# One third of a conditioning matrix in two halves, and another third moved to the end of the layer before

## The chip, the cores and the metric

The kernel runs on one core of a Trainium2 chip. The metric is the device time of one execution in microseconds (us); the median of three runs of the kernel before is 1125.9 us (1125.2 to 1128.83).

## The reference: what is computed

Two layers over 640 tokens (512 latent, 128 context) of width 1024. Cut to what matters here:

```python
mod = silu(c) @ w_ada[l] + b_ada[l]          # one row for latent, one for context: 6*1024 columns
shift1, scale1, gate1, shift2, scale2, gate2 = split(mod, 6)
h = rms_norm(x, norm1) * (1 + scale1) + shift1
proj = h @ w_in                              # 1024 -> 2048, then attention, gating MLP, convolution
x = x + gate1 * (merged @ w_out)
h2 = rms_norm(x, norm2) * (1 + scale2) + shift2
x = x + gate2 * hierarchical_moe(h2, ...)    # two experts of sixteen for each token
```

The weight `w_ada[l]` is 1024 x 6144 floats, 25 MB a layer. Its columns are used in three thirds: the first is shift1 and scale1 (wanted before the layer's first matmul), the second gate1 and shift2, the third scale2 and gate2 (wanted after the attention).

## The kernel before

All work is written out by hand, one instruction stream for each engine, ordered by semaphores; there is no planner. Tokens are five tiles of 128 (four latent, one context). Float32 products are made of three passes (`three`, L1421 to L1423): weights and activations are split into a high and a low part (ScalarE makes `wH`, `actH`; VectorE `wL`, `actL`).

**The weight stream.** `STREAM` lists the 1 MB units of w_ada ("ada"), w_in and w_out ("w") in the order in which SP loads them. They share four buffers (`raw`, RAWS = 4), so unit i+4 is issued only when unit i has been read (`unit_used`). SP is one queue in program order; parameter loads, convolution shifts and expert loads stand in the same queue.

**A modulation unit** (`ada_mm`, L1439) is four matmuls of a 128 x 32 slice of silu(c) with 512 columns each, into four groups of 32 rows of one PSUM bank. Eight units make a third. VectorE adds the bias (`piece_add`, or `half_add` after each four units), GpSimd loads the biases (`bias_in`, four DMAs) and writes finished thirds to memory (`piece_out`, L495). For the first third TensorE transposes the sums to columns (`modc_cols`, L1447) and VectorE makes shift and scale columns `modc` of it (`modc_out`, L1002 and L1007).

**Start of layer 0.** SP loads four units, then an x tile with each further unit, all eight units ahead of w_in. ScalarE squares the five x tiles (L639), scales them (L645), then splits the first w_in unit (L659). TensorE transposes x (`h_chunk`, L1463); ScalarE applies the columns (L676, L678, L681) and VectorE makes the low part (L1035) for each of eight k-tiles; then the projection runs k-tile by k-tile, 15 matmuls each for the first 512 columns.

**Attention** goes over 40 heads (`u`, five tiles of eight; the context tile comes first as tile 0 with only 128 keys). `ADA_AT` puts the second and last third of the layer's modulation, 16 units, among the heads: four in each of the tiles 0 to 3, at heads 2 to 5. `HALF_AT` puts VectorE's bias additions (L993, L996) at the last head of each of these tiles.

**End of layer 0.** After the experts GpSimd gathers two rows for each token (`y1`, `y2`, ten indirect DMAs of 512 KB, L619). ScalarE scales the first (L946); VectorE combines and adds to x, tile by tile (L1403 to L1405); ScalarE squares and scales x for the next layer. SP's first four loads of layer 1 (w_in units) wait for the fourth tile's gathers (`y_in3`). The first third of layer 1's modulation has been computed earlier, in front of and among the routing of layer 0.

Of the kernel before, what the change touches and what calls it, by code (L numbers as in the profile page):

```python
# [16 lines left out]
P = 128  # L17
D = 1024
# [66 lines left out]
def build(nc, I, O):  # L85
    with ExitStack() as ctx:
# [112 lines left out]

        rt = pool[:, 11264:13312]  # L200
# [41 lines left out]
        ADA_AT = (0, 0, 1, 1, 1, 1, 0, 0) * NLT + (0,) * NH  # L242
        HALF_AT = {8 * t + 7: t for t in range(NLT)}
# [3 lines left out]
        def ada_bank(l, q):  # L247

            return 7 if q else 6 if l else 5
# [22 lines left out]
        def unit_loaded(eng, kind, l, n):  # L272
            i = POS[kind, l, n]
            eng.wait_ge(s_raw[i % RAWS], 16 * (i // RAWS + 1))
# [12 lines left out]
        def _(sp):  # L287
# [30 lines left out]
            def load_taps(l):  # L318

                sp.wait_ge(sem("modc_psum"), at("modc_psum", l, 1))  # L320
# [4 lines left out]
            for l in range(DEPTH):  # L325
                for i in range(START[l], START[l + 1]):
                    kind, ll, n = STREAM[i]
                    if i == START[l] + (20 if l == 0 else 12):
# [31 lines left out]
                    k0, n0 = (n % 2) * 4, (n // 2) * N  # L360
                    if kind == "ada":
# [92 lines left out]
        def _(pl):  # L454
# [24 lines left out]

            def bias_in(l, q):  # L480

                if q == 1:
# [3 lines left out]
                for j in range(4):  # L486
                    c = q * U + j * N
                    pl.dma_start(bpiece[q][32 * j:32 * j + 32, :], I["b_ada"][l, c:c + N].partition_broadcast(32)).then_inc(sem("bias_in"), 16)

            def piece_out(l, q):  # L490

                pl.wait_ge(sem("piece_done"), at("piece_done", l, q + 1))
                for j in range(4):
                    c = q * U + j * N
                    pl.dma_start(modrow[l][:, c:c + N], piece[q][32 * j:32 * j + 2, :]).then_inc(sem("piece_out"), 16)  # L495
# [5 lines left out]
            bias_in(0, 0)  # L501
            rstd1(0)
            first = pairs = 0
            for l in range(DEPTH):
# [10 lines left out]
                bias_in(l, 1)  # L515
# [26 lines left out]
                piece_out(l, 1)  # L542
# [74 lines left out]
                for t in range(NT):  # L617
                    for c, y in enumerate((y1[t], y2[t])):
                        pl.indirect_dma_start(y, None, ys, bass.IndirectOffsetOnAxis(slot[:, c * NT + t:c * NT + t + 1], 0)  # L619
                                              ).then_inc(sem(f"y_in{t}"), 16)  # L620
                rstd1(l + 1)


        @block.scalar
        def _(act):
# [21 lines left out]
            for t in range(NT):  # L647
                act.wait_ge(sem(f"x_loaded{t}"), 16)
                norm1_square(0, t)
            for t in range(NT):  # L650
                norm1_scale(0, t)
            first = pairs = 0
            for l in range(DEPTH):
# [13 lines left out]

                split_hi(0)

                for k in range(KD):  # L670
                    act.wait_ge(sem("hT_psum"), at("hT_psum", l, k + 1))
                    if k == 0:
                        act.wait_ge(sem("a1_ready"), at("a1_ready", l, 1))
                    if k >= 2:
                        act.wait_ge(sem("h_lo"), at("h_lo", l, k - 1))
                    act.activation(hf[:, k % 2, 0:512], ps[:, 5 + 2 * (k % 2), :], ACT.Identity,  # L676
# [24 lines left out]
                for gi in range(4 * NT):  # L701
# [27 lines left out]
                    elif nb == 1:  # L729
                        j = t if t < CTX else CTXK  # L730
                        act.wait_ge(sem("ssqk"), at("ssqk", l, t + 1))
# [224 lines left out]
        def _(dve):  # L956
# [22 lines left out]
            def piece_add(l, q):  # L979

                dve.wait_ge(sem("ada_read"), at("ada_read", l, KD * (q + 1)))
                dve.wait_ge(sem("bias_in"), at("bias_in", l, 64 * (q + 1)))
# [4 lines left out]
            def half_add(l, i):  # L987

                q, half = 1 + i // 2, i % 2
                dve.wait_ge(sem("ada_read"), at("ada_read", l, KD * q + 4 * half + 4))  # L990
                if half == 0:
                    dve.wait_ge(sem("bias_in"), at("bias_in", l, 64 * (q + 1)))
                    dve.tensor_tensor(piece[q], ps[:, ada_bank(l, q), :], bpiece[q], ALU.add).then_inc(sem("piece_half"), 1)  # L993
                else:
                    dve.wait_ge(sem("piece_half"), at("piece_half", l, q))
                    dve.tensor_tensor(piece[q], ps[:, ada_bank(l, q), :], piece[q], ALU.add).then_inc(sem("piece_done"), 1)  # L996

            def modc_out(l):

                dve.wait_ge(sem("modc_psum"), at("modc_psum", l, 1))  # L1000
# [3 lines left out]
                dve.wait_ge(sem("modc_in"), 4 * (l + 1))  # L1004
                if l == 0:
                    dve.wait_ge(sem("norm1_loaded"), 16 * DEPTH)
# [10 lines left out]
            piece_add(0, 0)  # L1017
            modc_out(0)
            first = pairs = 0
            for l in range(DEPTH):  # L1020
# [12 lines left out]
                for k in range(KD):  # L1033
# [3 lines left out]
                    if k == 2:  # L1037
                        split_lo(1)
                split_lo(2)
# [757 lines left out]
```

## Time and profile before

| | us |
|---|---|
| median of three runs | 1125.9 |
| the profiled execution | 1123.17 |
| its span, first to last instruction | 1121.3 |
| TensorE busy | 937.7 (84%) |
| VectorE busy | 674.9 (60%) |
| ScalarE busy | 591.5 (53%) |
| GpSimd busy | 260.7 (23%) |

The page divides the span into 40 slices; in them the DMA engines carry over 400 GB/s while experts are loaded, and 10 to 250 in most others. TensorE is idle or nearly so in three places: the first 44 us, the stretch from 544 to 581 (end of layer 0) and the last 43 us. A stall of an engine off the chain of waits costs nothing by itself.

### The profile page before, as it was taken

To read this page: it belongs to the slowest core of one execution; us is meant where nothing else is said; L and a number is where in the kernel's file an instruction comes from. 1 tells how busy PE (TensorE), PEld (TensorE's weight loads), DVE (VectorE), ACT (ScalarE), POOL (GpSimd) and SP (SyncE) were. 2 spreads that over 40 slices of the span, in tenths; PEclk is the share of its full clock that TensorE was granted. 3 is DMA by queue.
4 is the path that set the end of the run, shared out by engine and by line. 5 is a ranking of instruction groups with operands and counts; after the bars stand their busy time and mean duration, and the time that the engine had idled before them with its cause. 6 is when DMAs were issued, how large, how long until landed. Compare 5 with 4: busy or idle time off the path is not lost.

```text
span 1121.3 us, 15024 instructions
## 1 busy us (share of the span) xinstructions
PE 937.7 (84%) x5232; PEld 733.4 (65%) x5232; DVE 674.9 (60%) x945; ACT 591.5 (53%) x913; POOL 260.7 (23%) x306
## 2 busy tenths in 40 slices
PE   3799998996999599999329999899789939999920
PEld 0488874765778278888218888467668838888710
DVE  0249315565264699999273941455725669998936
ACT  1662225565232288888275322556623418888732
POOL 3015006212041122220240410620203212222143
PEclk9999998999997699999759999999989959999975
DMA  9956216643153999999771240566313449999853
GB/s 318 285 184 245 75 59 222 242 152 115 56 216 113 381 332 406 418 413 369 185 283 43 77 149 10 202 236 226 113 58 132 158 155 347 400 421 405 342 196 122
DMA packets 85951, 248.36 MB, mean 221 GB/s; under 512 B 25644, under 2 KB 30252, under 8 KB 75656
## 3 DMA queue, kind: packets, MB, share of 16 engines
q1 hardware_dynamic: 72760, 209.54, 50.2%
q0 software_dynamic: 11696, 32.86, 8.5%
q10 hardware_dynamic: 1440, 5.24, 1.2%
q8 instruction: 33, 0.54, 0.2%
q14 instruction: 22, 0.18, 0.0%
HBM read 221.07 MB, written 30.21 MB: 224 GB/s over the span
## 4 chain that ended last, share of the span: by engine, by line
PE 68%; DMA 10%; DVE 10%; ACT 7%; issue 4%; POOL 1%; SPq 0%; ACTq 0%; POOLq 0%; DVEq 0%
PE ps L1421 12%; PE ps L1423 12%; PE ps L1422 12%; DMA pool<-in_moe_w 5%; PE ps L1439 4%; PE ps L1428 4%; PE ps L1430 4%; PE ps L1429 4%; PE ps L1557 3%; PE ps L1572 3%; PE ps L1546 2%; PE ps L1692 2%; ACT wH L856 2%; DVE wL L1227 2%; PE ps L1547 2%
## 5 line engine op out<-in xcount | busy, mean ns | idle before, releaser
L1421 PE MATMUL ps<-wH,actH 128*128 128x512 f32 x608 | 247.0, 406 | 6.8 <-DVE actL L1356 5.4
L1423 PE MATMUL ps<-wH,actL 128*128 128x512 f32 x608 | 240.7, 396 | 0.0
L1422 PE MATMUL ps<-wL,actH 128*128 128x512 f32 x608 | 239.7, 394 | 0.0
L1227 DVE TENSOR_TENSOR wL<-raw,wH 128x2048 fp32r<-128x2048 f32 x64 | 146.0, 2283 | 11.6 <-ACT wH L856 11.4
L856 ACT ACTIVATE wH<-raw 128x2048 fp32r<-128x2048 f32 x64 | 122.4, 1912 | 28.7 <-DMA raw<-in_moe_w 25.5
L1421 PEld LDWEIGHTS ps<-wH,actH 128*128 128x128 f32 x608 | 116.4, 191 | 31.9 <-issue 7.5
L1423 PEld LDWEIGHTS ps<-wH,actL 128*128 128x128 f32 x608 | 115.8, 190 | 25.9
L1422 PEld LDWEIGHTS ps<-wL,actH 128*128 128x128 f32 x608 | 116.4, 191 | 22.6
L1428 PE MATMUL ps<-wH,actH 128*128 128x512 f32 x256 | 105.2, 411 | 4.2 <-DVE wL L1227 2.8
L1430 PE MATMUL ps<-wH,actL 128*128 128x512 f32 x256 | 102.0, 398 | 0.0
L1429 PE MATMUL ps<-wL,actH 128*128 128x512 f32 x256 | 101.0, 395 | 0.0
L589 POOL DMA_INDIRECT pool<-h2s,idxc x28 | 50.6, 1806 | 195.5 <-PE ps L1692 181.0
L1153 DVE TENSOR_REDUCE nmax<-ps 128x1 f32<-128x640 f32 (+1 forms) x80 | 57.2, 714 | 58.1 <-PE ps L1547 58.1
L1439 PE MATMUL ps<-raw,cpad 128*32 128x512 f32 x384 | 62.8, 739 | 25.7 <-DMA raw<-in_w_ada 25.2
L1227 DVE TENSOR_TENSOR wL<-pool,wH 128x2048 fp32r<-128x2048 f32 x32 | 73.1, 2284 | 15.3 <-ACT wH L856 15.3
L802 ACT ACTIVATE pool<-ps,nmax 128x640 f32<-128x640 f32 (+1 forms) x80 | 56.6, 707 | 45.0 <-DVE nmax L1153 44.7
L856 ACT ACTIVATE wH<-pool 128x2048 fp32r<-128x2048 f32 x32 | 61.2, 1912 | 3.5 <-DMA pool<-in_moe_w 3.4
L1557 PE MATMUL ps<-ident,pool 128*128 128x128 f32 x336 | 53.3, 284 | 9.1 <-DVE tabs L1161 4.7
L1428 PEld LDWEIGHTS ps<-wH,actH 128*128 128x128 f32 x256 | 49.1, 192 | 15.6 <-DVE wL L1227 3.5
L659 ACT ACTIVATE wH<-raw 128x2048 fp32r<-128x2048 f32 x20 | 38.3, 1935 | 38.4 <-PE ps L1423 38.4
L892 ACT ACTIVATE actH<-ps 128x512 fp32r<-128x512 f32 x64 | 38.3, 598 | 37.8 <-PE ps L1692 35.2
L1023 DVE TENSOR_TENSOR wL<-raw,wH 128x2048 fp32r<-128x2048 f32 x20 | 45.5, 2290 | 18.5 <-ACT wH L659 18.3
(233 smaller groups left out, 1594.8 us busy)
## 6 DMA issues: line engine op xcount, KB each, us to landing
raw<-in_w_ada SPq DMA_DIRECT2D x48, 1024.0 KB, 5.1
raw<-in_moe_w SPq DMA_DIRECT2D x96, 512.0 KB, 8.1
raw<-in_w_in SPq DMA_DIRECT2D x16, 1024.0 KB, 8.4
raw<-in_moe_w SPq DMA_DIRECT2D x16, 1024.0 KB, 12.3
pool<-in_moe_w SPq DMA_DIRECT2D x32, 512.0 KB, 7.8
pool<-in_moe_w SPq DMA_DIRECT2D x16, 1024.0 KB, 11.7
ys<-pool SPq DMA_DIRECT2D x32, 512.0 KB, 10.7
raw<-in_w_out SPq DMA_DIRECT2D x8, 1024.0 KB, 5.2
```

Of the source, the lines that this page charges most:

```text
L802: act.activation(prob[:, u % 2, 0:keys], flat[:, 2 * N * (u % 2):2 * N * (u % 2) + keys], ACT.Exp, bias=nmax[:, u % 2:u % 2 + 1], accum_ou ...
L856: act.activation(wH[:, i if place is None else place, :], mraw[parity][i], ACT.Copy).then_inc(sem(f"m_hi{i}"), 1)
L1153: dve.tensor_reduce(nmax[:, u % 2:u % 2 + 1], flat[:, 2 * N * (u % 2):2 * N * (u % 2) + keys], X, ALU.max, negate=True).then_inc(sem("nmax ...
L1227: dve.tensor_tensor(wL[:, w, :], mraw[parity][i], f32(wH[:, w, :]), ALU.subtract).then_inc(sem(f"m_lo{i}"), 1)
L1421: pe.matmul(out, aH, wH[:, slot_, cols_], start=first, stop=False)
L1422: pe.matmul(out, aH, wL[:, slot_, cols_], start=False, stop=False)
L1423: return pe.matmul(out, aL, wH[:, slot_, cols_], start=False, stop=last)
L1428: pe.matmul(out, aH, hi, start=first, stop=False)
L1429: pe.matmul(out, aH, lo, start=False, stop=False)
L1430: return pe.matmul(out, aL, hi, start=False, stop=last)
L1439: m = pe.matmul(ps[32 * j:32 * j + 32, ada_bank(l, q), :], c32, raw[:, POS["ada", l, n] % RAWS, j * N:(j + 1) * N], start=(kt % group == 0 ...
L1557: m = pe.transpose(ps[:, 4 + c // 4, (c % 4) * P:(c % 4) * P + P], prob[:, w % 2, c * P:(c + 1) * P], ident[:, :])
```

## The change

In layer 0 the first third is split in two halves of its columns: four units hold the first 512 columns of shift1 and of scale1 for all 1024 rows, four the second 512. Each of these units is two DMAs with 2 KB rows. The first half is multiplied ahead of everything, the second among the first four k-tiles of the projection. The bias enters by a matmul with a row of ones, and the turn into columns is a matmul with a selecting matrix (`pick`). The columns of the k-tiles 4 to 7 come from the second half. x tiles and the first w_in unit are loaded earlier.

In layer 1 the second third (eight units) goes into the stretch after the experts of layer 0: its loads stand first in layer 1's stream, its matmuls after the last expert block, its bias addition after the last tile of the combination, and SP's wait for the gathers is gone. Layer 1's attention keeps the last third, at the tiles 1 and 2.

```diff
-STREAM, START = [("ada", 0, n) for n in range(8)], [0]
+STREAM, START = [("ada", 0, n) for n in range(3)] + [("w", 0, 0)] + [("ada", 0, n) for n in range(3, 8)], [0]
 for _l in range(DEPTH):
-    STREAM += [("w", _l, n) for n in range(8)] + [("ada", _l, n) for n in range(8, 24)] + [("w", _l, n) for n in range(8, 12)]
+    STREAM += [("ada", _l, n) for n in range(8, 16) if _l]
+    STREAM += [("w", _l, n) for n in range(int(_l == 0), 8)] + [("ada", _l, n) for n in range(16 if _l else 8, 24)] + [("w", _l, n) for n in range(8, 12)]
...
+        bspare, spare = pool[:, 11264:11776], pool[:, 12288:12800]
...
-        ADA_AT = (0, 0, 1, 1, 1, 1, 0, 0) * NLT + (0,) * NH
-        HALF_AT = {8 * t + 7: t for t in range(NLT)}
+        ADA_AT = [(0, 0, 1, 1, 1, 1, 0, 0) * NLT + (0,) * NH] + [(0,) * NH + (0, 0, 1, 1, 1, 1, 0, 0) * 2 + (0,) * (2 * NH)] * (DEPTH - 1)
+        HALF_AT = [{8 * t + 7: t for t in range(NLT)}] + [{15: 2, 23: 3}] * (DEPTH - 1)
...
-                sp.wait_ge(sem("modc_psum"), at("modc_psum", l, 1))
+                sp.wait_ge(sem("modc_psum"), at("modc_psum", l, 2))
...
                     if l > 0 and i < START[l] + RAWS:
                         sp.wait_ge(sem("moe_split_done"), at("moe_split_done", l - 1, 1))
-                        sp.wait_ge(sem(f"y_in{NT - 2}"), 32 * l)
...
-                    if 3 <= i < 3 + NT:
-                        t = i - 3
+                    for t in {1: (0,), 2: (1, 2), 3: (3,), 4: (4,)}.get(i, ()):
...
+                    if kind == "ada" and ll == 0 and n < KD:
+                        half, k2 = divmod(n, 4)
+                        for a in range(2):
+                            kt = 2 * k2 + a
+                            sp.dma_start(raw[:, i % RAWS, a * 2 * N:(a + 1) * 2 * N].rearrange("p (s c) -> p s c", s=2),
+                                         I["w_ada"][0, kt * P:(kt + 1) * P, 0:U].rearrange("p (s h c) -> p s h c", s=2, h=2)[:, :, half, :]
+                                         ).then_inc(s_raw[i % RAWS], 16)
+                        continue
...
+            pl.dma_start(brow, I["b_ada"][0, 0:U].rearrange("(a n) -> a n", a=1)).then_inc(sem("ident_loaded"), 16)
...
-            bias_in(0, 0)
             rstd1(0)
...
-                piece_out(l, 1)
+                if l == 0:
+                    piece_out(l, 1)
                 bias_in(l, 2)
...
+                if l + 1 < DEPTH:
+                    bias_in(l + 1, 1)
                 rstd1(l + 1)
+                if l + 1 < DEPTH:
+                    piece_out(l + 1, 1)
...
                     if k == 0:
-                        act.wait_ge(sem("a1_ready"), at("a1_ready", l, 1))
+                        act.wait_ge(sem("a1_ready"), at("a1_ready", l, 2 if l else 1))
+                    if k == 4:
+                        act.wait_ge(sem("a1_ready"), at("a1_ready", l, 2))
...
+            def first_sums(half):
+                dve.wait_ge(sem("ada_read"), 4 * half + 4)
+                dve.tensor_copy(piece[0], ps[:, 7, :]).then_inc(sem("piece_done" if half else "first_piece"), 1)
+            def first_cols(half):
+                dve.wait_ge(sem("modc_psum"), half + 1)
...
                     if k == 2:
                         split_lo(1)
+                    if l == 0 and k == 3:
+                        first_sums(1)
+                        first_cols(1)
...
-                    if u in HALF_AT:
-                        half_add(l, HALF_AT[u])
+                    if u in HALF_AT[l]:
+                        half_add(l, HALF_AT[l][u])
...
+                if l + 1 < DEPTH:
+                    dve.wait_ge(sem("ada_read"), at("ada_read", l + 1, 2 * KD))
+                    dve.wait_ge(sem("bias_in"), bias_count(l + 1, 1))
+                    dve.wait_ge(sem("ss1"), at("ss1", l + 1, NT))
+                    dve.tensor_tensor(spare, ps[:, ada_bank(l + 1, 1), :], bspare, ALU.add).then_inc(sem("piece_done"), 1)
...
-            for n in range(KD):
-                ada_mm(0, n)
-            modc_cols(0)
+            def first_bias(half):
+                for s_ in range(2):
+                    c = s_ * D + half * N
+                    pe.matmul(ps[32 * s_:32 * s_ + 32, 7, :], one32, brow[:, c:c + N], start=True, stop=False, skip_group_check=True)
+            def first_ada(n):
...
+            def first_shift(half):
+                pe.wait_ge(sem("piece_done" if half else "first_piece"), 1)
+                for i in range(4):
+                    m = pe.matmul(ps[:, 7, 4 * i:4 * i + 4], piece[0][:, i * P:(i + 1) * P], pick, start=True, stop=True, skip_group_check=True)
+                m.then_inc(sem("modc_psum"), 1)
+            first_bias(0)
+            for n in range(4):
+                first_ada(n)
+            first_shift(0)
...
+                        if l == 0 and nb == 0 and kt == 3:
+                            first_shift(1)
                         if nb == 0 and kt + 2 < KD:
                             h_chunk(kt + 2)
+                        if l == 0 and nb == 0 and kt < 3:
+                            if kt == 0:
+                                pe.wait_ge(sem("a1_ready"), 1)
+                                first_bias(1)
+                            first_ada(4 + kt)
+                            if kt == 2:
+                                first_ada(7)
...
-                        for j in range(sum(ADA_AT[:u]), sum(ADA_AT[:u + 1])):
-                            ada_mm(l, KD + j)
+                        for j in range(sum(ADA_AT[l][:u]), sum(ADA_AT[l][:u + 1])):
+                            ada_mm(l, (2 * KD if l else KD) + j)
...
+                if l + 1 < DEPTH:
+                    for n in range(KD, 2 * KD):
+                        ada_mm(l + 1, n)
```

## Rows read from the trace of the kernel before

**Rows 1.** Chain of waits at the start: start us, length us, what

```profile
34.07 5.20 ACT pool L645 x5
...
44.18 0.80 PE ps L1421
```

**Rows 2.** Stretches: length, busy us of each engine, granted clock, DMA share, GB/s

```profile
20.00:25.00 5.00, 2.79 (x13) 0.40 (x16) 0.00 (x0) 1.15 (x2) 0.74 (x2) 1.00 1.03 423
...
40.00:45.00 5.00, 2.80 (x11) 1.90 (x10) 3.03 (x3) 4.29 (x7) 0.00 (x0) 1.00 1.05 385
...
44.20:100.00 55.80, 55.80 (x250) 46.06 (x251) 31.13 (x46) 26.37 (x36) 14.85 (x12) 1.00 0.64 206
```

**Rows 3.** Timeline at the start: start us, length us, engine, line, operation [idle before]

```profile
27.91 1.94 PE L1439 MATMUL ps<-raw,cpad 128*32 128x512 f32 x8 [1.83 <-DMA raw<-in_w_ada]
...
37.51 0.69 DVE L985 TENSOR_TENSOR misc<-ps,misc 128x512 f32<-128x512 f32 x1 [27.32 <-PE ps L1439]
...
38.26 1.12 PE L1447 MATMUL ps<-ident,misc 128*128 128x128 f32 x4 [0.88 <-DVE misc L985]
...
39.41 0.38 DVE L1002 COPY modc<-ps 128x8 f32<-128x8 f32 x4 [1.21 <-PE ps L1447]
...
43.50 0.78 ACT L676 ACTIVATE pool<-ps,modc 128x512 f32<-128x512 f32 x1 [0.65 <-PE ps L1463]
...
45.42 0.82 DVE L1035 TENSOR_TENSOR actL<-pool,actH 128x640 fp32r<-128x640 f32 x1 [1.30 <-ACT actH L681]
...
50.06 0.71 PE L1463 MATMUL ps<-ident,pool 128*128 128x128 f32 x5
```

**Rows 4.** Timeline of TensorE in layer 1's attention

```profile
713.00 1.93 PE L1439 MATMUL ps<-raw,cpad 128*32 128x512 f32 x8
...
719.84 0.33 PE L1546 MATMUL ps<-actH,actL 128*128 128x128 f32 x1
...
720.71 0.33 PE L1546 MATMUL ps<-actH,actL 128*128 128x128 f32 x1
...
732.32 1.31 PE L1572 MATMUL ps<-pool 128*64 128x128 f32 x20
...
738.48 1.31 PE L1572 MATMUL ps<-tabs,pool 128*64 128x128 f32 x20
...
742.75 1.31 PE L1572 MATMUL ps<-pool 128*64 128x128 f32 x20
```

**Rows 5.** Timeline of GpSimd and VectorE there

```profile
740.73 0.56 POOL L531 TENSOR_TENSOR stat<-stat,nhalf 128x1 f32<-128x1 f32 x1
...
741.80 0.68 DVE L996 TENSOR_TENSOR misc<-ps,misc 128x512 f32<-128x512 f32 x1
...
745.06 2.00 POOL L488 DMA_DIRECT2D pool<-in_b_ada  x4
```

**Rows 6.** DMA issues there: count, KB each, median us from issue to landing

```profile
pool<-in_b_ada POOLq DMA_DIRECT2D x4, 64.0 KB, 2.3
```

**Rows 7.** Chain of waits at the end of layer 0

```profile
545.27 4.80 DMA ys<-pool
...
552.15 5.20 DMA pool<-ys,slot
...
558.73 1.30 DVE pool L1403
...
573.59 1.29 DVE pool L1403
...
580.56 1.90 ACT wH L659
```

**Rows 8.** Stretch after the experts of layer 0

```profile
545.00:550.00 5.00, 0.00 (x0) 0.00 (x0) 1.61 (x11) 1.70 (x4) 0.00 (x0) 0.76 0.67 256
```

**Rows 9.** DMA queues from 380 to 383.5 (experts): packets, MB, share of 16 engines

```profile
q1 hardware_dynamic: 275, 0.98, 69.6%
q0 software_dynamic: 218, 0.45, 33.5%
```

More of the change, by code:

```diff
@@ L273, in unit_loaded @@
             i = POS[kind, l, n]
-            eng.wait_ge(s_raw[i % RAWS], 16 * (i // RAWS + 1))
+            eng.wait_ge(s_raw[i % RAWS], 16 * sum(2 if STREAM[j][0:2] == ("ada", 0) and STREAM[j][2] < KD else 1 for j in range(i % RAWS, i + 1, RAWS)))
         def w_read(eng, l, i):
@@ L478, in row @@
                 return ap.partition_broadcast(P)
+            pl.dma_start(brow, I["b_ada"][0, 0:U].rearrange("(a n) -> a n", a=1)).then_inc(sem("ident_loaded"), 16)
             def bias_in(l, q):
-                if q == 1:
+                if q == 1 and l == 0:
                     pl.wait_ge(sem("sgT_psum"), at("sgT_psum", l, 1))
@@ L487, in bias_in @@
                     c = q * U + j * N
[L488 removed]
+                    pl.dma_start((bspare if q == 1 and l else bpiece[q])[32 * j:32 * j + 32, :], I["b_ada"][l, c:c + N].partition_broadcast(32)).then_inc(sem("bias_in"), 16)
             def piece_out(l, q):
@@ L494, in piece_out @@
                     c = q * U + j * N
-                    pl.dma_start(modrow[l][:, c:c + N], piece[q][32 * j:32 * j + 2, :]).then_inc(sem("piece_out"), 16)
+                    pl.dma_start(modrow[l][:, c:c + N], (spare if q == 1 and l else piece[q])[32 * j:32 * j + 2, :]).then_inc(sem("piece_out"), 16)
             def rstd1(l):
@@ L666, in quarter_hi @@
                                    ).then_inc(sem("quarter_hi"), 1)
+                if l == 0:
+                    for t in range(NT):
+                        act.wait_ge(sem(f"x_loaded{t}"), 16)
+                        norm1_square(0, t)
+                        if t:
+                            norm1_scale(0, t - 1)
+                    norm1_scale(0, NT - 1)
                 split_hi(0)
@@ L730, in _ @@
                         j = t if t < CTX else CTXK
+                        if l and t == 0:
+                            act.wait_ge(sem("piece_out"), at("piece_out", l, 64))
                         act.wait_ge(sem("ssqk"), at("ssqk", l, t + 1))
@@ L1015, in final_norm @@
                                          op0=ALU.mult, op1=ALU.mult).then_inc(sem("y_final"), 1)
-            piece_add(0, 0)
-            modc_out(0)
+            dve.wait_ge(sem("ident_loaded"), 32)
+            dve.memset(one32, 1.0).then_inc(sem("upper_ready"), 1)
+            pairs_of = [ident[:, 64 * a:64 * a + 64].rearrange("p (s r) -> p s r", s=2)[:, :, 0:2] for a in range(2)]
+            dve.tensor_tensor(pick.rearrange("p (s c) -> p s c", s=2), pairs_of[0], pairs_of[1], ALU.add).then_inc(sem("upper_ready"), 1)
+            def first_sums(half):
[3 more added lines that the diff above has]
+                dve.wait_ge(sem("modc_psum"), half + 1)
+                dst = modc[:, :, :].rearrange("p (s h i) c -> p h i s c", s=2, h=2)[:, half]
+                dve.tensor_copy(dst, ps[:, 7, 0:16].rearrange("p (i s c) -> p i s c", i=4, s=2)).then_inc(sem("modc_in"), 1)
+                dve.wait_ge(sem("modc_in"), half + 1)
+                if half == 0:
+                    dve.wait_ge(sem("norm1_loaded"), 16 * DEPTH)
+                k0 = KD + 4 * half
+                dve.scalar_tensor_tensor(out=modc[:, k0:k0 + 4, :], in0=modc[:, k0:k0 + 4, :], scalar=1.0,
+                                         in1=bc(cols[:, k0:k0 + 4], 2), op0=ALU.add, op1=ALU.mult
+                                         ).then_inc(sem("a1_ready"), 1)
+            first_sums(0)
+            first_cols(0)
             first = pairs = 0
@@ L1434, in ada_mm @@
                 q, kt = divmod(n, KD)
-                group = 4 if q else KD
+                group = 4 if q == 2 or q and l == 0 else KD
                 unit_loaded(pe, "ada", l, n)
@@ L1448, in modc_cols @@
                 m.then_inc(sem("modc_psum"), 1)
-            for n in range(KD):
-                ada_mm(0, n)
-            modc_cols(0)
+            def first_bias(half):
[3 more added lines that the diff above has]
+            def first_ada(n):
+                half, k2 = divmod(n, 4)
+                unit_loaded(pe, "ada", 0, n)
+                for a in range(2):
+                    kt = 2 * k2 + a
+                    for s_ in range(2):
+                        j = 2 * a + s_
+                        m = pe.matmul(ps[32 * j:32 * j + 32, 7, :], cpad[:, 2 * kt:2 * kt + 32], raw[:, POS["ada", 0, n] % RAWS, j * N:(j + 1) * N],
+                                      start=(a == 1 and k2 == 0), stop=(k2 == 3), skip_group_check=True)
+                m.then_inc(sem("ada_read"), 1)
+            def first_shift(half):
[3 more added lines that the diff above has]
+                m.then_inc(sem("modc_psum"), 1)
+            pe.wait_ge(sem("ident_loaded"), 32)
+            pe.wait_ge(sem("upper_ready"), 5)
+            first_bias(0)
+            for n in range(4):
+                first_ada(n)
+            first_shift(0)
             first = pairs = 0
@@ L1486, in _ @@
                             pe.wait_ge(sem("h_lo"), at("h_lo", l, kt + 1))
+                            if l and kt == 0:
+                                pe.wait_ge(sem("piece_done"), at("piece_done", l, 2))
                         if k == 0:
```

47 lines of the change are left out of this document (29 added, 18 removed).

## The prediction, made before the changed kernel was run

> **What bounds the kernel now.** I read the page first (TensorE busy in most slices of the span, except three troughs: the start, the end of layer 0 and the end of layer 1), then the chain of waits at the start and at the end of layer 0, then the timeline and the stretches there, and last the attention of layer 1. At the start the chain runs over the loads, then over ScalarE's five scalings of x (34.07 to 39.27), and the first projection matmul starts at 44.18 [rows 1]. From there TensorE is busy 55.80 of 55.80 us [rows 2]: whatever is put between those matmuls costs its own length. At the end of layer 0 the chain is the last store of expert results (545.27), the gathers, five tiles of VectorE work and the weight split at 580.56 [rows 7]; TensorE has nothing to do there. In the attention of layer 1 a pair of heads takes 6.16 us with two modulation units among it (732.32 to 738.48) and 4.27 without (to 742.75) [rows 4]: 0.95 us a unit, on the path.
>
> **Part one, the start.** *Removed:* four of the eight units from ahead of the first matmul. Up to its start on the sixth unit at 27.91 [rows 3], TensorE had received six units and three x tiles, 7.86 MB; that is just what the new order loads up to its fourth unit (four units, five x tiles, one w_in unit). So that unit would come at 27.9, corrected for its pieces. The new units arrive in pieces of 2 KB; w_in, in such pieces, moved at 385 GB/s where the 8 KB rows and x moved at 423 [rows 2]: 5.24 MB cost 1.2 us more. The bias broadcast that went (0.26 MB) gives 0.6 back: 28.5. The Trainium skill ("DMA: Bandwidth & Descriptors", Specifications) gives 512 B as the smallest transfer at full rate. By that the 1.2 us would not be there and the start 1.2 us earlier; this trace disagrees, and I keep 385.
>
> Then, each from [rows 3]: the unit 1.94 to 30.4, VectorE's copy 0.69 (the old addition's time), four small matmuls 1.12 (the old transposes'), columns and scale 0.6 (the four copies took 0.38 and one more operation follows) to about 33.0, five transposes 0.71 at full clock and so some 1.4 at half. Then ScalarE's and VectorE's work on a chunk: 43.50 to the end of 45.42+0.82, 2.74. The first matmul starts at 36.5 instead of 44.18: a gain of 7.7. The last x tile comes one unit before (25.8); its square and scale (1.04 each by the five in 5.20 [rows 1]) and the 1.9 us split end by 31, beside this. Bounds: 6 (small matmuls and bias row late) to 9.5 (no cost of small pieces, fourth unit at the earliest).
>
> *Added among the first projection:* four units at 0.95 = 3.8 and the bias matmuls, half a unit, 0.5. After the fourth k-tile the second half's columns are wanted: four small matmuls (0.6 at full clock, as five transposes take 0.71), columns 0.6 with its hand-over, one chunk 2.74 and hand-overs 0.2. TensorE waits there 4.2 where five transposes stood (0.57 of their 0.71 was net): 3.6. Behind the waiting matmul stands all of TensorE; ScalarE's h of k=4 waits for the same columns, VectorE is free. Sum 7.9. Bounds 6.5 (the wait partly met by earlier columns) to 10.5 (the clock falls to half during the wait, as it did in a stretch in which TensorE had nothing: mean 0.76 [rows 8]; a few us at half speed cost two more). The second w_in unit now waits for the fifth modulation unit's slot; by the same steps it is in about 0.6 us before its rows are wanted: nothing, but close. SP's parameter loads wait for the second columns (some 12 us later); the weights behind them are wanted 30 us later still. **Part one: +0.3, from -3 to +4.5.**
>
> **Part two, attention of layer 1.** Eight of sixteen units leave. In the tile 3 four units: two pairs at 6.16-4.27 = 3.8 us. In tile 0 four heads with a unit each took 713.00 to 719.84, 6.84; the head after took 0.87 [rows 4], which would save 3.3. But the first unit took 1.93, so TensorE's clock was at its lower level there, and without units the tile is sparser and may stay at it; 1.5 at that end, and I take 2.0, nearer to the half-clock row. *A new wait:* the only piece left is added to its bias at head 15 instead of 23. Its bias is issued by GpSimd after the statistic that ended at 741.29 (740.73+0.56): four issues over 2.0 us, the last landing 2.3 us after its issue, 745.1; VectorE's addition of head 15 stood at 741.80 [rows 5, 6]. VectorE waits 3.3 with the reductions of head 16 behind it, and TensorE, which would have come to its next transposes at 742.75+1.31 = 744.06 [rows 4], gets them at 745.1+0.7+0.1: 1.9. Bounds 0 to 3.5. **Attention: -2.0-3.8+1.9 = -3.9, from -7 to -1.5.**
>
> **Part three, the combination of layer 0.** *Moved in:* eight 1 MB loads (8.39 MB), ahead of the w_in units, with no wait for the gathers any more. SP issues the first four behind the last store at 545.27 [rows 7]. Until the gathers flow (552), the engines are free for 160 GB/s up to 550 (256 of 416 used [rows 8]) and fully for two more: 1.5 MB. From there 6.9 MB stand against ten gathers of 0.524 MB. TensorE reads a unit in 1.94, faster than one arrives, so SP's queue is never empty. How the queues share: over 3.5 us with both at work, the gathers' queue had 33.5% of the engines, SP's 69.6% (0.45 and 0.98 MB; 218 and 275 packets) [rows 9]. A third of 416 is 139 GB/s for gathers, 277 for units. The units end at 552+24.9 = 577; a tile's two gathers (1.05 MB) take 7.55 us. Tiles 0 to 2 land at 560.6, 568.1, 575.7 (1 us each for the tail). Then SP's pieces are 2 KB against 4 KB, which I take as two thirds for the gathers: tile 3 at 580.6, tile 4 at 584.4. Before, tile 0 landed at 557.35, VectorE began 1.38 later and took 3.72 a tile (558.73 to 573.59 for four) [rows 7]. Now tile 3 ends at 585.7 and tile 4 at 589.4; it was 577.3. **+12.1.** What follows (square, scale, split, transposes) keeps its length. The one addition (0.7) after the last square, the eight units on an idle TensorE and four bias issues on GpSimd (2.0 us in all [rows 5]) lie beside VectorE's tiles: nothing.
>
> Bounds: with equal shares (208 GB/s) tile 4 lands at 578.2 and ends at 583.3, +6.0. With the gathers served first, the 13.2 MB left at 552 (units, gathers, one w_in unit) end at 583.7, where the split stood at 580.56: +3. I take the third, since the row is the only one in which several gathers stand against a full queue.
>
> **Sum.** +0.3-3.9+12.1 = +8.5 on the profiled execution's 1123.2 (1121.3 of span and 1.9 around it): 1131.7. The median of the runs is 2.7 above the profiled one, 1125.9: **1134.4**.
>
> **The rivals.**
> *Equal turns by bytes.* Combination +6.0: sum +2.4, 1128.3. For: an 8 KB row may be split in turns. Against: [rows 9].
> *Gathers first, not slower:* place, 552 to 581. If the gathers hold more than two thirds of the engines (282 GB/s, 1.05 MB in 3.72 us), VectorE's tiles stay where they are and only the w_in unit is late: +3-3.9+0.3 = -0.6, 1125.3. It decides from that share on. For: ten gathers queue at once. Against: the third seen.
> *Everything added in the first projection is cheaper than I count* (lower bound 6.5, gain 9.5: -3) on top of equal or better shares: -3-3.9+3 to 6 = -4 to -1, 1122 to 1125; the faster half is what the change says it is. For: TensorE's units are short. Against: the wait after the fourth k-tile has no cover.
> *The clock falls* in that wait, and tile 0 of layer 1's attention stays at half clock: +8.5+2.6+0.5, 1137.5.
>
> **How the numbers follow.** Forecast 0.52, equal turns 0.18, gathers first 0.10, cheap addition 0.10, clock 0.10. A measurement of this kernel tells about 0.3% (3.4 us) from no change. The cheap addition with the best shares and some of gathers first give faster 0.12; the rest of these and most of equal turns 0.20; slower 0.68. The range goes from 1123 (gathers first, with part one near its lower end) to 1142 (the clock, with a late second w_in unit); the forecast's own is 1129 to 1140.
>
> **What would show it.** First projection matmul near 36.5, then a gap of about 4 us after its fourth k-tile, its fifth starting near 62.5 as before. In layer 1's attention VectorE idle about 3 us at head 15 for the bias. At the end of layer 0 ScalarE's scalings of the gathered rows 6 to 8 us apart instead of about 3, and the w_in split near 593. Wrong, if those scalings keep their places (rival two), or if the fifth k-tile starts before 60 or after 66.

## The result, and the profile after

The changed kernel takes 1141.6 us (median of four runs, 1137.4 to 1146.9) against 1126.6 for the kernel before: a ratio of 1.0137 (1.0108 to 1.0166), some 15 us slower where 8.5 were forecast. The direction and its main cause were right, and the time lies at the upper edge of the range (1142); the size was not.

The chain of waits of the changed kernel over the end of layer 0 and the start of layer 1 (start us, length us, what). It answers to [rows 7]:

```profile
545.23 1.03 ACT pool L962
546.42 5.86 DMA ys<-pool
...
553.10 0.96 POOL pool L652
...
564.31 26.46 DMA pool<-ys,slot
590.80 1.16 ACT pool L992
...
599.03 1.90 ACT wH L691
600.96 2.29 DVE wL L1091
604.04 0.80 PE ps L1498
```

The 26.46 us of the last gather are the line to look at: in [rows 7] the chain left the gathers after the first tile and went over five tiles of VectorE's work; now it waits for the last tile's rows. ScalarE's last scaling of expert results ended at 546.26 here. In the kernel before it ended at 545.10; of that kernel's chain, three more links:

```profile
544.07 1.03 ACT pool L916
...
550.89 0.96 POOL pool L619
...
585.57 0.79 PE ps L1421
```

From the end of that scaling to layer 1's first projection matmul it took 40.5 us before (to 585.57) and takes 57.8 now: **17.3 us more**. I use this stretch below, because profiled executions of one kernel differ elsewhere.

ScalarE's timeline there shows when each of the five tiles of gathered rows was there (start us, length us, engine, line, operation [idle before]):

```profile
565.47 1.15 ACT L992 ACTIVATE pool<-pool,gate 128x1024 f32<-128x1024 f32 x1 [17.59 <-DMA pool<-ys,slot]
572.97 1.15 ACT L992 ACTIVATE pool<-pool,gate 128x1024 f32<-128x1024 f32 x1 [6.35 <-DMA pool<-ys,slot]
579.97 1.15 ACT L992 ACTIVATE pool<-pool,gate 128x1024 f32<-128x1024 f32 x1 [4.81 <-DMA pool<-ys,slot]
585.66 1.15 ACT L992 ACTIVATE pool<-pool,gate 128x1024 f32<-128x1024 f32 x1 [2.47 <-DMA pool<-ys,slot]
590.80 1.15 ACT L992 ACTIVATE pool<-pool,gate 128x1024 f32<-128x1024 f32 x1 [1.91 <-DMA pool<-ys,slot]
```

They are 7.5, 7.0, 5.7 and 5.1 us apart, where VectorE needs 3.7 a tile [rows 7]. The DMA queues of the changed kernel from 553.1 to 557.1 us, and then from 558 to 560 (q1 is SP's, q0 GpSimd's; packets, MB, share of 16 engines):

```profile
q1 hardware_dynamic: 225, 1.66, 100.0%
```

```profile
q1 hardware_dynamic: 75, 0.54, 64.0%
q0 software_dynamic: 75, 0.31, 37.3%
```

Although the first gather was issued at 553.10, nothing of it flows until after 557.1. Then both queues send the same number of packets, and since a unit's packets are rows of 8 KB and a gather's rows of 4 KB, the gathers have a third.

At the start, the chain of the changed kernel up to the first projection matmul, which answers to [rows 1], and TensorE's timeline around the fifth k-tile:

```profile
26.86 1.98 PE ps L1541 x8
...
29.61 1.87 PE ps L1549 x8
...
35.49 0.79 PE ps L1498
```

```profile
58.28 0.95 PE L1549 MATMUL ps<-misc 128*128 128x4 f32 x8
60.91 0.76 PE L1568 MATMUL ps<-ident,pool 128*128 128x128 f32 x5 [1.68 <-ACT pool L722]
62.53 0.50 PE L1498 MATMUL ps<-wH,actH 128*128 128x512 f32 x1 [0.86 <-DVE actL L1103]
```

The first matmul is 8.7 us earlier than in [rows 1], and the fifth k-tile begins at 62.53, as forecast to the tenth: the gain is given back.

In layer 1's attention, the waits of the changed kernel from 755 to 772 us (who waits for whom: total us, times, longest):

```profile
DVE pool L1040 <- DMA pool<-in_b_ada: 4.5, 1, 4.5
PE ps L1643 <- DVE pool L1040: 3.0, 1, 3.0
```

VectorE waits for the bias rows (L1040 is the addition of the bias), and TensorE for VectorE. Of the chain there, from the statistic on GpSimd that the bias rows are issued behind:

```profile
759.42 0.56 POOL stat L563
...
761.53 3.42 DMA pool<-in_b_ada
...
765.04 0.70 DVE pool L1040
...
765.79 0.66 PE ps L1643 x4
```

### The profile page after: what moved, and what is told of

It is laid out like the page before. It is cut to its first block, busy times and chain, and to the rows that moved or that the text cites. A ratio compares the mean times of both kernels' runs of the same rounds, so it can differ in the third digit from the quotient of the medians.

```text
span 1145.0 us, 15067 instructions
## 1 busy us (share of the span) xinstructions
PE 954.7 (83%) x5252; PEld 744.7 (65%) x5252; DVE 675.2 (59%) x946; ACT 591.4 (52%) x913; POOL 253.2 (22%) x303
## 4 chain that ended last, share of the span: by engine, by line
PE 66%; DMA 12%; DVE 9%; ACT 6%; issue 4%; POOL 2%; SPq 0%; ACTq 0%; POOLq 0%; DVEq 0%
PE ps L1498 12%; PE ps L1500 12%; PE ps L1499 12%; PE ps L1505 4%; PE ps L1507 4%; PE ps L1506 3%; PE ps L1675 3%; PE ps L1516 3%; DMA pool<-ys,slot 3%; DMA raw<-in_moe_w 3%; DMA pool<-in_moe_w 3%; PE ps L1690 3%; PE ps L1664 2%; DVE wL L1298 2%; PE ps L1815 2%
## 5 line engine op out<-in xcount | busy, mean ns | idle before, releaser
L1298 DVE TENSOR_TENSOR wL<-raw,wH 128x2048 fp32r<-128x2048 f32 x64 | 146.0, 2283 | 12.6 <-ACT wH L902 12.2
L1516 PE MATMUL ps<-raw,cpad 128*32 128x512 f32 x320 | 51.1, 725 | 25.1 <-DMA raw<-in_w_ada 24.8
L1505 PEld LDWEIGHTS ps<-wH,actH 128*128 128x128 f32 x256 | 49.2, 192 | 16.5 <-DVE wL L1298 4.7
```

The source lines that it names most:

```text
L1298: dve.tensor_tensor(wL[:, w, :], mraw[parity][i], f32(wH[:, w, :]), ALU.subtract).then_inc(sem(f"m_lo{i}"), 1)
L1505: pe.matmul(out, aH, hi, start=first, stop=False)
L1516: m = pe.matmul(ps[32 * j:32 * j + 32, ada_bank(l, q), :], c32, raw[:, POS["ada", l, n] % RAWS, j * N:(j + 1) * N], start=(kt % group == 0 ...
```

## The experiments

There are two theories of the extra cost at the end of layer 0. *Turns*: the queues alternate packet by packet, so the gathers are starved by their shorter rows. *Volume*: gathers, eight units and the first w_in unit (14.7 MB) must land before the projection in whatever order. The kernel before moved this from 546 to 583 us (packets, MB, mean rate):

```profile
DMA packets 3919, 10.39 MB, mean 281 GB/s; under 512 B 263, under 2 KB 373, under 8 KB 3918
```

Some 415 GB/s over 37 us would be 15.4 MB, so 5.0 MB are free there. Another 3.1 MB are w_in units 2 to 4, not yet wanted. The change adds 8.4 MB.

**One part at a time.** The first two kernels each leave one part out: part one alone takes layer 1 from the kernel before, part two alone takes the start from it. In short:

```diff
 # part one alone
-    STREAM += [("ada", _l, n) for n in range(8, 16) if _l]
-    STREAM += [("w", _l, n) for n in range(int(_l == 0), 8)] + [("ada", _l, n) for n in range(16 if _l else 8, 24)] + ...
+    STREAM += [("w", _l, n) for n in range(int(_l == 0), 8)] + [("ada", _l, n) for n in range(8, 24)] + ...
...
 # part two alone
-STREAM, START = [("ada", 0, n) for n in range(3)] + [("w", 0, 0)] + [("ada", 0, n) for n in range(3, 8)], [0]
+STREAM, START = [("ada", 0, n) for n in range(8)], [0]
```

> Part one alone: the first layer's first third in two halves, layer 1's second third left where the kernel before has it. Theory A (the start gains 8 to 9 us at the first matmul and gives it back in the first projection, since the four units, the bias matmuls and the wait after the fourth k-tile stand there): the fifth k-tile within 0.3 us of the kernel before, and the whole within 1 us of it, 1125.5 to 1127.5. Rival B (part one carries a part of the 15 us, through the doubled loads or a later state of the loads in layer 0): 1129 or more. Rival C (part one is a gain that part two hides): 1123 or less.

Measured: 1129.3 us beside 1128.7 for the kernel before on that chip, ratio 1.0002 (0.998 to 1.0024). In microseconds this meets rival B's bound of 1129, but the kernel before ran higher beside it too, and the ratio decides: theory A holds. The fifth k-tile began at 61.64 (before: 62.51), so not within the 0.3 us asked for, but the whole is unchanged.

> Part two alone: layer 1's second third loaded and computed beside layer 0's combination, the start as before. Theory A (the whole cost is part two's): 1139 to 1143, the split of layer 1's first projection 17 to 19 us later than before, and the attention of layer 1 1 us shorter at most. Rival B (the cost needs both parts): 1134 or less.

Measured: ratio 1.0113 (1.0065 to 1.0161), 1139.6 us. The whole cost is part two's, as A said; rival B falls. The stretch to the first projection matmul was 55.8 us (545.20 to 601.04), 15.4 longer than before, somewhat less than A's 17 to 19.

**Shorter rows for the units.** The count that the readers of a unit wait for is raised to match (not shown).

```diff
+                        if ll and q == 1:
+                            for j in range(4):
+                                sp.dma_start(raw[:, i % RAWS, j * N:(j + 1) * N],
+                                             I["w_ada"][ll, kt * P:(kt + 1) * P, q * U + j * N:q * U + (j + 1) * N]).then_inc(s_raw[i % RAWS], 16)
+                            continue
```

> The changed kernel with each of layer 1's eight moved units loaded as four transfers whose rows are 2 KB, in place of one transfer with rows of 8 KB; bytes, order and matmuls are the same. Theory A (the two queues take turns packet by packet, so the gathers, with rows of 4 KB, get 4/(4+2) = two thirds beside 2 KB rows in place of 4/(4+8) = one third): y tiles 4 to 5 us apart in place of 7, the eight units landing later, layer 1's first projection 6 to 12 us earlier than in the changed kernel, the whole 1130 to 1136. Rival B (bytes alone decide, the sum of unit and gather bytes must land before the projection whatever the shares): same as the changed kernel within 2 us, 1138 to 1143. Rival C (more transfers cost their issue and a lower rate): 1143 or more.

Measured: ratio 1.0079 (1.0054 to 1.0105). The queues of this kernel from 558 to 560 us, and three links of its chain:

```profile
q0 software_dynamic: 149, 0.54, 69.0%
q1 hardware_dynamic: 148, 0.27, 35.7%
```

```profile
580.03 8.80 DMA raw<-in_w_in
588.86 1.92 ACT wH L696
...
593.88 0.80 PE ps L1503
```

Again equal packets, 149 and 148, and now two thirds for the gathers: one edit of the row length turns the shares round, with bytes and order the same. Tiles came 3.9 us apart (559.96, 563.82, 567.73, 571.64, 575.74), the last one 31.1 us after ScalarE's last scaling instead of 44.5. Theory A holds for the shares. But the first projection matmul gained only 8.5 us of these 13.4 (49.2 us after that scaling, against 57.8): the chain no longer names the gathers, it waits for the w_in unit behind the units. From ScalarE's scaling to the landing of that unit (544.64 to 588.83) the DMA engines moved, without a pause:

```profile
DMA packets 7851, 16.97 MB, mean 384 GB/s; under 512 B 812, under 2 KB 1314, under 8 KB 7851
```

That is 2.3 MB more than the 14.7 listed above (a store of expert results, bias rows and the w_in units behind the first are among it), and at 384 GB/s instead of 415. Volume is the next bound, 8.8 us above the kernel before.

**The changed kernel again**, beside the three that follow:

> The changed kernel again, unedited, beside the three below on one chip. Every theory: 1.011 to 1.016 times the kernel before. If it falls to 1.008 or less, the early bias row of the earlier experiment was worth less than its seven microseconds.

Measured: ratio 1.0140 (1.0116 to 1.0163). Its stretch to the first matmul was 56.1 us (543.15 to 599.23), 15.6 longer than before; so the change costs 15.4 to 17.3 us there in three profiled executions (part two alone, this one and the first). With part one alone, where the combination is the old one, the stretch was 41.3 us (547.09 to 588.43), and 39.7 in the last part-one run below (543.60 to 583.28), against 40.5: it is known to about 1 us.

**The wait for the gathers put back.**

```diff
                         sp.wait_ge(sem("moe_split_done"), at("moe_split_done", l - 1, 1))
+                        sp.wait_ge(sem(f"y_in{NT - 2}"), 32 * l)
```

> The changed kernel with SyncE's wait for the fourth tile of gathers put back ahead of layer 1's loads: the gathers run alone as in the kernel before, and the eight moved units and the first w_in unit follow them. Theory A (contention: the change would cost little in the combination if the gathers were left alone): y tiles land as before (the fifth 15 to 18 us after the first gather's issue), but then 9 MB at 0.42 MB a us take 21 us after about 565, so the w_in unit lands near 588 to 590 and the first projection starts 8 to 11 us later than in the kernel before, against 18 in the changed kernel; the whole 6 to 9 us below the changed kernel. Rival B (volume: gathers, units and w_in have to land one after the other or together, 14.6 MB at any order): the projection within 3 us of the changed kernel's, the whole within 3 us.

Measured: ratio 1.0110 (1.0085 to 1.0134), 3.5 us below the unedited kernel, and not beyond doubt so. The chain of this kernel:

```profile
586.45 8.14 DMA raw<-in_w_in
...
594.61 1.92 ACT wH L692
...
599.64 0.79 PE ps L1499
```

The gathers were left alone, and the fifth tile was scaled at 573.98; yet the first matmul stands 53.5 us after ScalarE's scaling, 13.0 more than before. I had expected 8 to 11. Beside the unedited kernel on the same chip the first matmul gained 2.6 us, within rival B's 3. Loads that follow one another cost nearly what the sharing costs. Volume explains most of the loss here, and A's saving was overstated.

**The third unit held until the first tile is there.**

```diff
                         sp.wait_ge(sem("moe_split_done"), at("moe_split_done", l - 1, 1))
+                        if i >= START[l] + 2:
+                            sp.wait_ge(sem("y_in0"), 32 * l)
```

> The changed kernel, but the third of the moved units is not issued until the first tile of gathered rows has landed; two units go out as before. Theory A (the gathers' first data come 4.1 us after their issue in place of 1.8 because the unit queue is full at that time, and this late start is the part of the cost that the forecast left out): first data within 2.5 us of the issue, first tile 4 to 6 us earlier than in the changed kernel, later tiles again 7 us apart, the first projection 3 to 6 us earlier, the whole 3 to 6 us below the changed kernel. Rival B (the lost share only moves: units that start later take their third from the later tiles, and w_in comes later): the first tile earlier, but the fifth tile and the projection within 2 us of the changed kernel.

Measured: ratio 1.0075 (1.0038 to 1.0111). The tiles were scaled at 559.52, 561.99, 566.69, 574.23 and 582.66, and the first matmul came 50.1 us after ScalarE's scaling: 6 to 7.7 us better than the unedited kernel, more than A's 3 to 6. Rival B falls. SP's queue from the first gather's issue (552.38) to 554.8, and both queues in the tenth of a microsecond after that:

```profile
q1 hardware_dynamic: 128, 0.94, 97.4%
```

```profile
q1 hardware_dynamic: 7, 0.04, 97.7%
q0 software_dynamic: 1, 0.00, 26.1%
```

The first gathered row moved about 2.5 us after the issue, just where A put it. In the changed kernel it was 4.1 (issue 553.10, first packet between 557.1 and 557.2), in the kernel before 1.6 (550.89, first packet between 552.5 and 552.6). So two units out instead of four take 1.6 us off the late start. From the issue to the scaling of the first tile it took 7.1 us instead of 12.4 to 12.6, so the larger part of what the first tile gained, 3.7 us, came from sharing less (from 556 to 558 us the gathers' queue had 97.0% of the engines). A's reason is right in part: the late start is one part of the cost, the lost share another. The later tiles, 2.5, 4.7, 7.5 and 8.4 us apart, were not all 7 apart as expected.

**The w_in unit ahead of the last three units.** The 2 KB rows are in this kernel too (edit not shown again).

```diff
-    STREAM += [("ada", _l, n) for n in range(8, 16) if _l]
-    STREAM += [("w", _l, n) for n in range(int(_l == 0), 8)] + ...
+    STREAM += [("ada", _l, n) for n in range(8, 13)] + [("w", _l, 0)] + [("ada", _l, n) for n in range(13, 16)] if _l else []
+    STREAM += [("w", _l, n) for n in range(1, 8)] + ...
```

> The changed kernel with the moved units in transfers of 2 KB rows, as in the earlier experiment, and layer 1's first w_in unit put in the queue ahead of the last three of them. Theory A (with 2 KB rows the gathers no longer bind, and the projection waits for the w_in unit that stands last in the queue): the split starts when the combination ends, about 2 to 4 us earlier than with 2 KB rows alone, the last moved unit and its sum become the last, and the whole is 1 to 4 us below the earlier experiment's ratio of 1.0079, that is 1.004 to 1.007. Rival B (the last unit merely takes the w_in unit's place, 2.7 us of load and 2 us of matmul for one another): ratio 1.007 to 1.009.

Measured: ratio 1.0058 (1.0034 to 1.0082). The median lies in A's range, but the interval reaches into B's, so the time does not decide. The chain does:

```profile
581.92 7.40 DMA raw<-in_w_ada
589.37 1.94 PE ps L1521 x8
591.30 1.27 PE ps L1573 x5
...
595.40 0.50 PE ps L1503
```

ScalarE split the w_in unit from 584.2, but the projection waits for the last unit, with TensorE's transposes queued behind its matmuls: 6.0 us from the unit to the first projection matmul, which stands 49.8 us after ScalarE's scaling (49.2 without this edit). So it is rival B: one load takes the other's place.

**The bias issued before the statistics.**

```diff
+                if l:
+                    bias_in(l, 2)
                 rest_stats(0)
                 attn_stats(0)
                 if l == 0:
                     piece_out(l, 1)
-                bias_in(l, 2)
+                    bias_in(l, 2)
```

> The changed kernel, but in layer 1 GpSimd issues the bias rows of the last third before the attention statistics of the first tiles, not after them. Theory A (the wait for the bias at the first half sum, 3.4 us in the chain of waits, stands on the path): that wait is gone, the first unit of tile 2 comes 3 to 4.8 us earlier, the whole 2.5 to 5 us below the changed kernel. Rival B (the statistics, now later by two issues, or the loads' own wait take its place): within 1 us of the changed kernel.

Measured: ratio 1.0072 (1.0046 to 1.0098). This ran beside the row-length experiment, ahead of the rerun above. First and last product of probabilities and values in layer 1, in the kernel before, in the changed one, and with the early bias (durations in ns, first and last start in us):

```profile
L1572 PE MATMUL ps<-pool x168: 272/273/323, 716.9 to 811.5; 128*64 128x128 f32 x168
L1572 PE MATMUL ps<-tabs,pool x168: 272/273/476, 720.3 to 814.4; 128*64 128x128 f32 x168
```

```profile
L1690 PE MATMUL ps<-pool x168: 272/273/477, 734.9 to 830.2; 128*64 128x128 f32 x168
L1690 PE MATMUL ps<-tabs,pool x168: 272/273/473, 738.4 to 833.1; 128*64 128x128 f32 x168
```

```profile
L1692 PE MATMUL ps<-pool x168: 272/273/476, 732.9 to 824.5; 128*64 128x128 f32 x168
L1692 PE MATMUL ps<-tabs,pool x168: 272/273/472, 736.8 to 827.4; 128*64 128x128 f32 x168
```

From first to last these are 97.5, 98.2 and 94.5 us: the attention without the wait is 3.7 us shorter, and the waits for the bias are gone from the view. Theory A holds. The ratios of the runs give 7 us (4 either way), more than the trace shows; I keep the trace's 3.7. One such stretch varies by more than 1 us: with the attention of the kernel before it was 97.5 to 99.1 in three profiled executions, with the late bias 98.2 to 99.4 in seven. With the early bias it was 94.5 here and 94.0 in the last kernel below, so the gain is well outside that.

**Part one with its second half a k-tile earlier.**

```diff
-                    if l == 0 and k == 3:
-                        first_sums(1)
-                        first_cols(1)
+                    if l == 0 and k == 2:
+                        first_sums(1)
+                    if l == 0 and k == 3:
+                        first_cols(1)
...
-                        if l == 0 and nb == 0 and kt == 3:
+                        if l == 0 and nb == 0 and kt == 2:
                             first_shift(1)
...
-                            first_ada(4 + kt)
-                            if kt == 2:
-                                first_ada(7)
+                            first_ada(4 + 2 * kt)
+                            first_ada(5 + 2 * kt)
```

> Part one alone (as in the first experiment), with the second half of the first third one k-tile earlier: two units after the first k-tile and two after the second, the copy of the sums before the fourth k-tile's split on VectorE, the turn into columns after the third k-tile. Theory A (part one came out at nothing because the wait after the fourth k-tile, 3.6 us, and 4 units with their bias matmuls give back what the first matmul gains): the wait is gone, the fifth k-tile 2.5 to 4 us earlier than in part one alone, ratio to the kernel before 0.996 to 0.998. Rival B (the units' loads land too late for two of them after the first k-tile, and the wait moves to the first k-tiles): within 0.2% of the kernel before, with PE waiting for w_ada units near 45 us.

Measured: ratio 0.9978 (0.9957 to 1.0). Stretch 56 to 66 us of part one alone, and of this kernel (length, busy us of PE, PEld, DVE, ACT, POOL, granted clock, DMA share, GB/s):

```profile
56.00:66.00 10.00, 7.46 (x33) 5.99 (x32) 2.00 (x4) 3.73 (x6) 0.00 (x0) 0.83 0.81 144
```

```profile
56.00:66.00 10.00, 10.00 (x51) 8.26 (x50) 1.84 (x3) 5.49 (x9) 0.00 (x0) 1.00 0.76 113
```

TensorE's pause and the fall of its clock after it are gone. The fifth k-tile begins at 59.59 instead of 61.64, although this execution stayed at the lower clock some 2.6 us longer in the first k-tile (to 40.55 instead of 37.97). That is 2.1 us where 2.5 to 4 were expected; the ratio is within A's range.

**All of it together.** This kernel has four of the edits shown: 2 KB rows, the w_in unit ahead of the last three, the early bias, the earlier second half.

> The changed kernel with all that the earlier runs found put right together: 2 KB rows for the moved units and the w_in unit ahead of the last three (1.0058 alone), the bias rows of the last third before the statistics (worth 0.35% by its wait of 3.4 to 4 us, 0.65% by the two ratios), the start one k-tile earlier (0.3%). Theory A (the three add up): 0.997 to 1.001 times the kernel before, and not below part one early alone, as moving eight units costs 9 us at layer 1's first matmul and gives back 5 to 6 in the attention. Rival B (they overlap, since the loads bound all of it): 1.003 or more. Rival C (the moved units pay once the gathers are left alone): 0.995 or less, below part one early alone.

Measured: ratio 1.0003 (0.9979 to 1.0028): A. The 15 us that the change costs are gone when its bias wait, its start and its shares are mended, but no more than gone: its stretch to the first matmul is still 50.1 us (543.17 to 593.27), 9.6 above the kernel before. Part one early alone, without part two, is the fastest of the kernels run, at the edge of what can be told from the kernel before.

## Why the forecast fell short

**Part one: right.** Forecast +0.3, measured alone +0.02% (-0.2% to +0.24%). That the fifth k-tile came at 62.53, as forecast to the tenth, is partly luck, for two misses cancel. The gain was 8.7 for 7.7: the fourth unit was multiplied from 26.86 where 28.5 was forecast, and from there to the first matmul it took 8.6 instead of 8.0 (the sum has the five transposes at 0.71, though it names 1.4; they took 1.18). It was not the pieces that were faster, since from 20 to 28 us, mostly in rows of 2 KB, the loads moved at 390 GB/s, near the 385 taken; but from 12 to 16 us they moved at 403, where the kernel before had 301. What was added took 8.7 for 7.9. The wait after the fourth k-tile gives back a part of it: without that wait the fifth k-tile came 2.1 us earlier.

**The combination: the mechanism right, the term of +12.1 mis-sized.** The third for the gathers and the two thirds once the pieces are 2 KB were as forecast (from 578 to 580 us 138 packets of the gathers stood beside 137 of SP's, 64.9% and 37.7% of the engines), and the tiles' spacing was near it (7.5, 7.0, 5.7 and 5.1 us for 7.5, 7.6, 4.9 and 3.8); the row-length experiment shows the cause. What failed is "Tiles 0 to 2 land at 560.6, 568.1, 575.7": I let the gathers flow at 552, as in the kernel before. In the profiled execution the gathers' issue came 1.0 us later after ScalarE's scaling (6.84 against 5.79: the store landed in 5.86 instead of 4.80, with units behind it); the first tile was there 12.4 us after the issue, where my 560.6 was 9.7 after it (its first rows moved 4.1 us after the issue instead of 1.6); and the later tiles were spaced 25.3 us in all, not 23.8. 12.1+1.0+2.7+1.5 = 17.3, what was measured. In the changed kernel's second run the spacing was 23.8 as forecast, the issue 0.7 later and the first tile 2.9 later than forecast against its issue: 12.1+0.7+2.9 = 15.7 of 15.6. So the late start, of the issue and of its first rows, is most of the miss in one and all of it in the other. It goes with the units that stand in SP's queue: about 4 us behind four of them, whether their rows are 8 or 2 KB, and 2.5 behind two. Why rows wait that long there stays open.

**The attention of layer 1: forecast -3.9, measured about 0.** Tile 3 gave 4.7 (forecast 3.8) and tile 0 0.9 (forecast 2.0: TensorE stayed at its lower clock there, with 0.50 granted from 731 to 742 us, where the kernel before had 1.00 from 715; the bound of 1.5 allowed for that, but the measured 0.9 lies below it). The step that failed is the bias wait, "gets them at 745.1+0.7+0.1: 1.9". The order was as I put it, but the bias took 4.97 us from the end of the statistic (759.98) to its landing (764.95) instead of 3.8, and TensorE waited 3.0 instead of 1.9: for the last of four issues I had taken the median landing of 2.3 us, and it landed in 3.42. Behind the wait TensorE's clock was lower (0.63 granted from 766 to 768 us, 0.51 from 768 to 770), which the sum had left out: 9.6 us between two products (761.44 to 771.01) against 4.8 without the wait (742.75 to 747.54), so the wait cost 4.8. The early-bias run gives 3.7 of it back. With +4.8 in place of +1.9, and 4.7 and 0.9 in place of 3.8 and 2.0, the sum is -0.8; over the profiled executions no gain can be told from nothing.

The rest of the 23.7 us between the two profiled executions is spread over later stages whose code did not change. From layer 1's first matmul to the end, part one alone took 541.8 us and the kernel before 535.7, although this part of both is the same code and their medians agree; the changed kernel's profiled execution, 1146.9, is also the highest of its four times. So only 15 us are to be explained: 15.4 to 17.3, and nothing from the attention.

Of the rivals, *gathers first* and *equal turns by bytes* are refuted by the equal packets, and the cheap addition by the 8.7 us that was added. *The clock falls* was partly so: after the wait at the fourth k-tile, matmuls took 0.63 instead of 0.39 for a while, but in a part whose whole cost is nil; in tile 0 of the attention it was so too, and the bias wait brought a third fall that no rival had.

## What to carry to other kernels

Before loads are moved into a stretch, count its free bytes: here 5 MB, with 3 more that could be put off, against 8.4 added. By that count the change is 0.3 MB over, under 1 us; yet the best of the orders tried cost 8.8 us, as another 2.3 MB passed in the same stretch and all of it at 384 GB/s instead of 415 (an estimate from these numbers gives 6 us for the one and 3 for the other). So count everything that moves there, at the rate of the row length used. Then ask in what row lengths the queues meet: here the longer rows took the larger share, and the gathers fared best beside short rows or an empty queue. And a wait that is moved earlier by removed work is priced by its issue and landing under the new timing, with the slower clock behind it; here it was enough to issue the small load ahead of what it was queued behind.

## What the runs showed of the hardware

- Two queues with work sent equal numbers of packets at both row lengths tried: 75 and 75 with 8 KB against 4 KB rows, 149 and 148 with 2 KB against 4 KB. [Rows 9] had only hinted at it.
- A gather issued behind four units in the other queue moved its first packet 4.1 to 4.4 us after the issue in seven profiled executions, with 8 KB rows (553.10 to 557.2; 551.76 to 555.9 in part two alone) as with 2 KB rows (550.99 to 555.2), though 230 to 240 packets of that queue moved in between with the long rows and 850 to 940 with the short. Behind two units it was 2.5 (552.38 to 554.9), and 1.6 to 1.7 in four executions without units there (550.89 to 552.5 in the kernel before).
- Loads mostly in rows of 2 KB moved at 390 GB/s from 20 to 28 us of the changed kernel; the kernel before, with rows of 8 and 4 KB, moved 418 in the same time.
- The kernel before itself ran between 1120.6 and 1133.5 us in 22 runs beside one experiment, a wider spread than the 1125.2 to 1128.8 that the forecast stood on. The profiled execution alone (1123.2) is no measure of a difference of a few us in a stage that the change does not touch.
